# Copying half of each inverse level with ScalarE instead of GpSimd, under a new order of the delta rule's steps

## The reference, cut to what matters

```python
A = jnp.where(tril_strict, jnp.einsum('bhncd,bhnsd->bhncs', kb, k) * decay, 0.0)
rhs = jnp.concatenate([v * beta[..., None], kb * jnp.exp(G)[..., None]], axis=-1)
sol = lax.linalg.triangular_solve(eye + A, rhs, left_side=True, lower=True, unit_diagonal=True)
u, w = sol[..., :Dv], sol[..., Dv:]
...
v_new = u_n - jnp.einsum('bhck,bhkv->bhcv', w_n, state)
o_n = (jnp.einsum('bhck,bhkv->bhcv', q_n, state) + jnp.einsum('bhcs,bhsv->bhcv', qk_n, v_new))
state = state * gl_n[..., None, None] + jnp.einsum('bhck,bhcv->bhkv', k_n, v_new)
```

## Time and profile before

| | us |
|---|---|
| median of 3 runs | 2349.05 |
| lowest and highest run | 2348.51, 2350.01 |
| the profiled execution's own time | 2346.54 |
| its span, first to last instruction | 2344.3 |
| PE busy | 2147.7 |
| DVE busy | 1152.3 |
| ACT busy | 429.9 |
| POOL busy | 124.7 |

### The profile page before, as it was taken

How to read it: one execution, slowest core, us unless ns; L and a number is a source line. 1 busy time by engine, 2 the same in 40 slices (tenths; PEclk the granted TensorE clock), 3 DMA queues, 4 the chain that set the end, 5 groups by cost and what they waited for, 6 DMA issues and landing times.

```text
span 2344.3 us, 24167 instructions
## 1 busy us (share of the span) xinstructions
PE 2147.7 (92%) x8982; PEld 1311.8 (56%) x8982; DVE 1152.3 (49%) x2111; ACT 429.9 (18%) x885; POOL 124.7 (5%) x159
## 2 busy tenths in 40 slices
PE   7998888999999999998899999999997899999883
PEld 4444444888888744434444488888854333433331
DVE  4684563766676523487442457875436312121113
ACT  1114442101100010114210144520110000000003
POOL 0000000000000000000000033400000000000000
PEclk8998988999999999999999999999997899999996
DMA  7126510522122312121112100032352899999994
GB/s 273 36 82 244 191 40 1 153 72 101 43 102 96 109 41 108 36 72 36 36 59 85 36 1 1 1 133 83 109 207 101 359 428 426 426 426 426 427 424 188
DMA packets 97291, 364.67 MB, mean 156 GB/s; under 512 B 10397, under 2 KB 19282, under 8 KB 84626
## 3 DMA queue, kind: packets, MB, share of 16 engines
q1 hardware_dynamic: 86337, 340.62, 37.7%
q0 software_dynamic: 8720, 20.89, 2.4%
q10 hardware_dynamic: 2112, 1.57, 0.2%
HBM read 357.00 MB, written 17.57 MB: 160 GB/s over the span
## 4 chain that ended last, share of the span: by engine, by line
PE 75%; DVE 13%; DMA 6%; issue 3%; ACT 2%; ACTq 0%; SPq 0%; DVEq 0%; POOL 0%; POOLq 0%
PE bank L717 50%; PE bank L1492 8%; PE bank L1487 5%; PE bank L782 3%; PE bank L1195 2%; DMA mem<-in_w_gate 2%; DMA mem<-in_w_down 2%; PE bank L952 2%; DMA mem<-in_w_up 2%; DVE mem L2068 1%; PE bank L827 1%; DVE mem L2067 1%; ACT mem L2471 1%; PE bank L1468 1%; DVE mem L1726 1%
## 5 line engine op out<-in xcount | busy, mean ns | idle before, releaser
L717 PE MATMUL bank<-mem 128*128 128x256 f32 (+7 forms) x4736 | 1381.4, 453 | 29.4 <-ACT mem L2471 12.8
L717 PEld LDWEIGHTS bank<-mem 128*128 128x128 f32 (+1 forms) x4736 | 881.4, 193 | 467.2 <-issue 346.8
L1492 PE MATMUL bank<-mem 128*64 128x512 f32 x1248 | 283.9, 610 | 32.9 <-DMA mem<-in_w_gate 11.5
L1492 PEld LDWEIGHTS bank<-mem 128*64 128x64 f32 x1248 | 94.4, 140 | 212.7 <-issue 199.4
L2471 ACT ACTIVATE mem<-bank 128x512 f32<-128x512 f32 (+6 forms) x265 | 134.4, 507 | 367.1 <-PE bank L717 152.7
L782 PE MATMUL bank<-mem 128*128 128x128 f32 (+1 forms) x692 | 116.4, 301 | 51.9 <-DVE mem L1726 24.6
L2407 DVE TENSOR_TENSOR mem<-mem,bank 128x512 f32<-128x512 f32 x19 | 13.1, 690 | 276.0 <-PE bank L1492 203.5
L782 PEld LDWEIGHTS bank<-mem 128*128 128x128 f32 (+1 forms) x692 | 86.2, 151 | 101.3 <-DVE mem L1726 37.6
L1487 PE MATMUL bank<-mem 128*128 128x512 f32 x288 | 132.0, 614 | 6.8 <-ACT mem L2740 4.1
L1487 PEld LDWEIGHTS bank<-mem 128*128 128x128 f32 x288 | 55.2, 195 | 78.7 <-issue 70.1
L2584 ACT ACTIVATE mem<-bank 128x512 f32<-128x512 f32 (+1 forms) x50 | 29.1, 582 | 372.1 <-PE bank L717 370.4
(11 more groups left out here) (348 smaller groups left out, 1691.5 us busy)
## 6 DMA issues: line engine op xcount, KB each, us to landing
mem<-in_w_gate SPq DMA_DIRECT2D x37, 2048.0 KB, 22.6
mem<-in_w_up SPq DMA_DIRECT2D x37, 2048.0 KB, 25.0
mem<-in_w_down SPq DMA_DIRECT2D x36, 2048.0 KB, 25.7
mem<-in_w_in SPq DMA_DIRECT2D x18, 2048.0 KB, 7.8
mem<-in_w_ada SPq DMA_DIRECT2D x12, 2048.0 KB, 8.1
mem<-in_w_out SPq DMA_DIRECT2D x4, 2048.0 KB, 13.1
mem<-in_w_ple_gate SPq DMA_DIRECT2D x2, 2048.0 KB, 7.8
mem<-in_w_br_att SPq DMA_DIRECT2D x2, 2048.0 KB, 8.1
```

The source lines that it names most:

```text
L717: last = pe.matmul(o, l, r, start=(i == 0), stop=(i == len(pairs) - 1))
L1492: last_ = pe.matmul(o[here, :], lhs[:, k, here], w[:, k, cols], start=(k == 0), stop=(k == kk - 1))
```

## The change

GpSimd no longer copies the untouched half. ScalarE does, with an ACTIVATE of function Copy, in step `lower`, at the same kind of place in the list. GpSimd's copy in `first_inverse` stays and signals a semaphore of its own (`odd_moved`); `lower_moved` now counts five a chunk instead of six. TensorE waits for both. The table of times is new in all its entries, which changes the order of the steps on every engine. In chunk 2, for example, the list from the result of chunk 1 on now goes (TensorE's steps): result a1, result_turned b0, A_turned b2, result b1, turn 0 a, filler, turn 0 b, update 0 a, filler, update 0 b, turn 1 a, qk a, turn 1 b, update 1 a, qk b, turn 2 a, update 1 b, update 2 a, turn 2 b, turn 3 a, v_rows a, update 2 b, update 3 a, turn 3 b, turn 4 a, v_rows b, update 3 b, qk_turned a, update 4 a, turn 4 b, k_rows a, qk_turned b, turn 5 a, update 4 b, gains a3, k_rows b, turn 5 b, gains b3, update 5 a, q_state a, update 5 b, w a, q_state b, keys a3, u a, w b, w_state a, state a, keys b3, result_turned a1, u b, w_state b, A_turned a3, state b, result a.

Between turn 1 of a0 and turn 1 of a3 there were five fillers and now there are four; behind the last result there was one and now there are two.

```diff
--- before.py
+++ after.py
@@ -72,18 +72,19 @@
 SEQUENCE += range(MAIN, BLOCKS)
 
 
-DELTA_PERIOD, DELTA_LAG = 953, 58
+DELTA_PERIOD, DELTA_LAG = 976, 44
 DELTA_TIMES = (
-    ("spread", 0, -932), ("gains", 0, -328), ("decay", 0, -304), ("keys", 0, -236),
-    ("first_inverse", 0, -231), ("A_turned", 0, -90), ("mask", 0, -42), ("turn", 0, 100), ("lower", 0, 122),
-    ("update", 0, 181), ("mask", 1, 206), ("lower", 1, 211), ("qk", 0, 220), ("turn", 1, 229),
-    ("v_rows", 0, 233), ("mask", 2, 239), ("update", 1, 249), ("turn", 2, 303), ("mask", 3, 318),
-    ("lower", 2, 350), ("qk_turned", 0, 350), ("update", 2, 360), ("turn", 3, 373), ("lower", 3, 416),
-    ("mask", 4, 421), ("update", 3, 425), ("lower", 4, 445), ("turn", 4, 481), ("k_rows", 0, 491),
-    ("update", 4, 537), ("turn", 5, 574), ("update", 5, 612), ("w", 0, 633), ("u", 0, 643),
-    ("q_state", 0, 671), ("w_state", 0, 684), ("state", 0, 713), ("result", 0, 889), ("norm_squares", 0, 941),
-    ("norm_root", 0, 1082), ("norm_inverse", 0, 1276), ("norm", 0, 1366), ("result_turned", 0, 1476))
-FILLER_TIMES = (-1863, -150, 12, 154, 839, 1160, 1506, 2119, 2815, 4055)
+    ("spread", 0, -473), ("gains", 0, -421), ("decay", 0, -309), ("keys", 0, -266),
+    ("first_inverse", 0, -243), ("A_turned", 0, -189), ("mask", 0, -150), ("lower", 0, -142),
+    ("turn", 0, -114), ("mask", 1, -26), ("update", 0, 132), ("turn", 1, 260), ("lower", 1, 264),
+    ("qk", 0, 268), ("update", 1, 309), ("mask", 2, 327), ("turn", 2, 341), ("lower", 2, 357),
+    ("mask", 3, 366), ("update", 2, 383), ("turn", 3, 400), ("mask", 4, 404), ("v_rows", 0, 427),
+    ("lower", 3, 436), ("update", 3, 439), ("turn", 4, 465), ("lower", 4, 469), ("qk_turned", 0, 497),
+    ("update", 4, 506), ("k_rows", 0, 527), ("turn", 5, 547), ("update", 5, 637), ("q_state", 0, 658),
+    ("w", 0, 692), ("u", 0, 731), ("w_state", 0, 737), ("state", 0, 744), ("result", 0, 798),
+    ("norm_squares", 0, 829), ("norm_root", 0, 979), ("norm_inverse", 0, 1135), ("norm", 0, 1383),
+    ("result_turned", 0, 1742))
+FILLER_TIMES = (-1409, -179, -103, -11, 1139, 1664, 1861, 2093, 4027, 4286)
 
 
 def delta_order():
@@ -477,6 +478,7 @@
         x0_ready = [sem(f"delta_first_inverse{g}") for g in range(2)]
         level_ready = [sem(f"delta_level_masked{g}") for g in range(2)]
         scaled_ready = [sem(f"delta_decay_times_beta{g}") for g in range(2)]
+        odd_moved = [sem(f"delta_odd_columns_moved{g}") for g in range(2)]
         lower_moved = [sem(f"delta_lower_columns_moved{g}") for g in range(2)]
         squares_ready, lengths_summed, lengths_rooted = (sem(f"qk_{n}") for n in ("squares_ready", "lengths_summed", "lengths_rooted"))
         square_summed, square_rooted, result_ready = ([sem(f"delta_{n}{g}") for g in range(2)]
@@ -1298,7 +1300,9 @@
                         pe.wait_ge(x0_ready[g], ch + 1)
                     else:
                         pe.wait_ge(dve_free, mark["update", at_, lv - 1])
-                    pe.wait_ge(lower_moved[g], (LEVELS + 1) * ch + lv + 1)
+                    pe.wait_ge(odd_moved[g], ch + 1)
+                    if ch or lv:
+                        pe.wait_ge(lower_moved[g], LEVELS * ch + lv)
                     if lv < LEVELS:
                         X = B["inverse"][lv % 2]
                         half_turned(X)
@@ -2674,7 +2678,7 @@
 
             def delta_step(g, ch, name, lv):
 
-                B = delta[g]
+                B, at_ = delta[g], (g, ch)
                 if name == "decay":
                     decays(g, ch)
                 elif name == "A_turned":
@@ -2689,6 +2693,14 @@
                     four_out(B["XT"])
                     copy_out(B["u"][64:128, :, 0:64],
                              take()[64:128, 0:HG * 64].rearrange("p (a b) -> p a b", a=HG))
+                elif name == "lower":
+                    if lv == 0:
+                        act.wait_ge(x0_ready[g], ch + 1)
+                    else:
+                        act.wait_ge(dve_free, mark["update", at_, lv - 1])
+                    act.wait_ge(odd_moved[g], ch + 1)
+                    C(act.activation(next_inverse(B, lv)[:, :, :, 32:64], this_order(B["inverse"][lv % 2][:, 1]), ACT.Copy),
+                      lower_moved[g])
                 elif name == "qk_turned":
                     four_out(B["qkT"])
                 elif name == "u":
@@ -2789,10 +2801,10 @@
                 elif name == "first_inverse":
                     if ch:
                         pool.wait_ge(dve_free, mark["update", (g, ch - 1), LEVELS - 1])
-                        pool.wait_ge(lower_moved[g], (LEVELS + 1) * ch)
+                        pool.wait_ge(lower_moved[g], LEVELS * ch)
                     pool.tensor_copy(B["inverse"][0][:, :, :, 32:64],
                                      const("ident_odd", 2)[:, :, None, :].to_broadcast([P, 2, HG, 32]))\
-                        .then_inc(lower_moved[g], 1)
+                        .then_inc(odd_moved[g], 1)
                 elif name == "mask":
                     pool.wait_ge(act_free, mark["AT", at_])
                     if lv >= 2:
@@ -2803,15 +2815,6 @@
                                        level_order(B["AT"], lv)[:, :, half:2 * half, :],
                                        mask[:, None, :, :].to_broadcast([P, HG, half, 64 // half]), ALU.mult)\
                         .then_inc(level_ready[g], 1)
-                elif name == "lower":
-                    if lv == 0:
-                        pool.wait_ge(x0_ready[g], ch + 1)
-                        pool.wait_ge(act_free, mark["AT", at_])
-                    else:
-                        pool.wait_ge(dve_free, mark["update", at_, lv - 1])
-                    pool.wait_ge(lower_moved[g], (LEVELS + 1) * ch + lv + 1)
-                    pool.tensor_copy(next_inverse(B, lv)[:, :, :, 32:64], this_order(B["inverse"][lv % 2][:, 1]))\
-                        .then_inc(lower_moved[g], 1)
 
             for g in range(2):
                 decay_scaled(g, 0)
```

## The result

The changed kernel takes 2354.74 us (median of 14 runs, 2350.19 to 2359.49), the kernel before 2348.44 us (14 runs, 2343.83 to 2352.36). The ratio is 1.0029, with a 95% interval of 1.0020 to 1.0037. So it is 0.3% slower, a small loss but one clear of the noise. Forecast was 2346.7 us, 2.4 us faster; it is 6.3 us slower, just past the upper end of the range.

What follows compares the result with a forecast made beforehand. The stage was taken as a chain through TensorE, ScalarE and VectorE, with no engine full. Four stretches summed to -4.8 us, plus 2.4 for handovers: -2.4, so 2346.7 us; range 2344 to 2349.5, with first and third rival 2341.5 to 2354.5.

Steps and rivals of the forecast that it cites:

- As no one waits for them, this gives nothing directly.: GpSimd's forty copies, 22.3 us: nothing on the path waits for them, so moving them gains nothing directly.
- The first rival: The order works in full: handovers stay ideal and VectorE is relieved, -5.8 us, 2343.3 us; chance 0.25.
- The norm squares at 1.86 a set: VectorE ahead of turn 1 of a3: two sets of norm squares, 1.86 us each.
- 0.8 a chunk for stretched instructions: 0.8 us added for each of the three chunks with norms, for stretched VectorE instructions and handovers that aren't ideal.
- its 14.4 us: Level part, turn 1 to turn 5 of a2: forecast at 14.4 us, against 15.21 before.
- The relief of VectorE by 1 us: VectorE's instructions with two SBUF operands: 4.6 us stretched, of which the copies' leaving would free 1 us.
- 14.4 us of TensorE steps: Last stretch, behind turn 5 of a3: 14.4 us of TensorE steps, so result b is issued at 28.8.
- Filler only moved: VectorE bounds the middle, so a filler taken out gives back 0.9 us instead of 3.5; 2349.2 us, chance 0.16.
- The end: Behind the last result: two fillers and the first gate take 13.84 us; TensorE is late, no longer the weights.
- The copy: The moved 128x256 copy on ScalarE: 419 ns, with bounds of 275 and 632 ns.
- ScalarE becomes the bound: Ten copies lengthen each level part, ScalarE being 14.0 of 14.4 us full: 8.5 us more, 2355.2 us; chance 0.14.
- the 2.4 for handovers: 2.4 us added to the four stretches' -4.8 us, for the three chunks with norms.

Runs made afterwards that it cites:

- copy_paced: Kernel before with the copies on ScalarE in the old order, GpSimd keeping its old copies' waits for VectorE at their old places: 2351.11 us, ratio 1.0018.
- new_paced: Changed kernel with GpSimd keeping its copies' waits for VectorE, without the copies, at the new table's places: 2352.58 us, ratio 1.0024.
- order_alone: Kernel before with the new table of times, its copies left on GpSimd: 2354.03 us, ratio 1.0024.
- no_idle_wait: Changed kernel without TensorE's waits for v new in the last chunk's state step, which issues no matmul: 2349.75 us, ratio 1.0009.
- filler_back: Changed kernel with one filler taken from behind the last result back into the third stretch: 2352.60 us, ratio 1.0021.
- new_mended: Changed kernel with the filler put back, no waits in the last chunk's empty state step, and GpSimd's waits kept: 2346.61 us, ratio 0.9996.
- copy_alone: Kernel before with the copies on ScalarE and their semaphores, but the old table of times: 2355.39 us, ratio 1.0038.

## Why the prediction was wrong

**"As no one waits for them, this gives nothing directly."** This is the step that failed. It is true of TensorE's list of releasers, and says nothing about what stands behind the copies in their own queue. GpSimd's idle time before the copies was 27.0 us, 26.1 of it for L2174: for up to so long the masks behind them were held. The prediction read that row for the copies' length alone. The experiment that gives the waits back without the copies (copy_paced) shows 2.7 to 3.9 us of the copy's cost in the old order to be this, and 2.9 in the new one (new_paced), half clock included. The first rival's own objection, "masks stay, and run earlier, next to the norm squares", was the right mechanism, but it got no price.

**The norm squares at 1.86 a set, and 0.8 a chunk for stretched instructions.** They took 2.72 and 2.51 ahead of turn 1 of a3, 1.5 more together. In the level part of a2 three instructions beside masks lost 1.8 us: L2110 0.85 instead of 0.16, L2193 1.30 and L2114 1.19 instead of 0.69. That part was 1.4 over its 14.4 us in each of the chunks with norms (half clock aside), and 0.9 over its 14.0 in the first. The relief of VectorE by 1 us didn't come: its busy time is the same, as the masks were behind most of the stretched time and stayed. How much of the level part's 1.4 the stretched instructions explain is argued from the rows; waits of 0.3 us for ScalarE's copies lie in it too. In order_alone, the same order with GpSimd's copies, the part takes 14.9 in a1 and a2, so 0.9 of the 1.4 came with the copies' move to ScalarE. new_paced doesn't give them back (15.9): there five masks run back to back in the middle of the part, beside two wide instructions of 1.40 and 1.17.

**The last stretch, "14.4 us of TensorE steps" without a wait.** From turn 5 of a3 it was 16.8: two waits of 0.84 for v new and 0.7 more. In the old order a wait for v new stood there as well, once, 0.84 us ahead of the results; the new one has the empty step's on top, and the prediction had taken both for free. no_idle_wait shows the last stretch 2.3 us shorter without it.

**The clock wasn't considered.** It cost 1.9 us in the last stretch: both profiled executions of the program show it, and three kernels in which TensorE's idle time ahead of turn 1 of a3 is filled or shortened don't: TensorE is busy 3.2 of the 4 us ahead of it in filler_back and new_mended and 1.9 in new_paced, against 1.4 in the changed kernel. In the Trainium skill, "TensorE: Matmul & The Clock Gate", section "HAM oscillation — how this bites in real kernels", DMA waits between bursts of matmuls take the clock to half, and the next burst starts cold. The traces agree that idle time can do this, here waits for other engines (0.50 of full speed from inside the idle stretch on), but not that it must: in the two executions of copy_alone TensorE is busy the same 2.0 of the 4 us ahead of turn 1 of a3, and only one fell.

**"Filler only moved".** That rival said that a filler taken out of the third stretch gives back 0.9, not 3.46, since VectorE holds turn 1 there. filler_back measured 1.3. Its place and its size were right, but it was priced at 2.5 us over the forecast and the whole excess was 11.0.

**What held.** The end: 13.79 us from the last result to the next product against 13.84, TensorE late and not the load. The copy: 442 ns against 419.

**"ScalarE becomes the bound".** This rival ended near the measured time (2355.2), but that is luck: it wanted 2.1 us in each of four chunks from a full ScalarE, and ScalarE was not full (11.46 of 15.77 us). The 14.0 of 14.4 us that spoke for it had ten moved copies in a level part, which holds only eight, those of levels 1 to 4. The waits for the moved copy itself are 0.9 us in all. Its conditions were partly met, though. A copy with its gap takes 0.47 us, just over its 0.46, and copies are caught ahead of the other group's turn copies, which costs TensorE waits of 0.8 us in the changed kernel and 3.0 in copy_paced.

The sum, by where each excess over the forecast lies: 0.9 + 1.4 + 1.4 + 1.4 in the level parts, 1.9 of half clock, 0.7 + 1.0 + 2.2 behind turn 5 in the first three stretches, 2.4 in the last: 13.3, of which the 2.4 for handovers had been allowed. Of the 2.2 in the third stretch 1.5 are the norm squares; the other 0.7, the 0.7 of the first stretch and the 1.0 of the second were not taken apart further. Open too are the 4.1 us that copy_paced keeps over before, but for its one half clock and the waits for ScalarE.

## What to carry to other kernels

An instruction on which nobody waits may still be doing work by waiting itself: before moving it, read the idle time in front of its row, and ask what its queue will do earlier once that is gone, and beside whom. Where TensorE waits for another engine, spare work put into the gap is cheap (1.3 us for 3.46), can keep the clock up, and costs its whole length once it stands behind the last wait. When a step is empty for some index, see that its waits go with it.

## What the runs showed of the hardware

- Beside a run of GpSimd masks (0.8 to 0.9 us each), VectorE's products of two operands in SBUF and its TENSOR_SCALAR wait a mask out, however short they are: a 128x4 product went from 0.16 to 0.79 us, a 128x4 multiplication by constants from 0.17 to 0.78, a 128x512 product from 0.69 to 1.29 and 1.39. With masks back to back this hit one instruction after another, two or three in a row; a reduction of 128x512 beside the same masks stayed at 0.69, and so did products with an operand in PSUM. The Trainium skill, "SBUF — State Buffer", section "Who interferes with whom", has the reduction, and instructions with at most one SBUF operand outside the two-port modes, clear of the shared ports, and the product of two SBUF operands on them; the rows agree with all three. The TENSOR_SCALAR has one SBUF operand and was hit all the same; in which mode it ran no row shows. The rows add that the price, 0.6 to 0.7 us at either size, doesn't go by the size of VectorE's instruction; it is most of one mask.
- ScalarE copies 128x256 from SBUF to SBUF with a stride of two elements in 442 ns (40 of them, 431 to 453), against 387 for the same size from PSUM without the stride. Hardly any rate is lost to the stride.
- TensorE's clock fell to half in a stage in which the engine is busy nine tenths of the time, behind 4 us in which it was busy 2.6 us (0.8 in the last 2), and stayed there 6.8 us though the engine was fully busy again for the last 5.5 of them. In other kernels of this study it lasted 3.4 or 6.8 us. It doesn't follow every such gap: in the second execution of copy_alone TensorE was busy 2.0 of the 4 us ahead of turn 1 of a3 and idle for the last 2, and the clock stayed at 1.00; in new_paced it stayed at 1.00 behind 1.9 of 4.
